# Delta-rule stage of a two-block transformer kernel: blockwise inverse by substitution, folded q norm, an explicit order of steps

## The reference, cut to what matters

```python
proj = h @ w_in                                   # q, k, v, z and the two gates of a head
qkv = silu(causal_depthwise_conv(qkv, conv_w))
q = l2_norm(q) * 128 ** -0.5
k = l2_norm(k)
lower = where(strict, beta * (k @ k.T) * decay, 0)
u, w = triangular_solve(I + lower, [v * beta, k * beta * exp(g)])
v_new = u - w @ S                                 # chunk by chunk, S is carried on
o = q_dec @ S + (q @ k.T * decay) @ v_new
S = S * g_last + k_dec.T @ v_new
out = (rms_norm(o, o_gain) * silu(z)) @ w_out
```

## Time and profile before

| | us |
|---|---|
| median of 3 runs | 1770.11 (1769.47 to 1771.78) |
| the profiled execution's own time | 1770.35 |
| its span, first to last instruction | 1768.1 |

### The profile page before, as it was taken

How to read it: one execution, slowest core, us unless ns; L and a number is a source line. 1 busy time by engine, 2 the same in 40 slices (tenths; PEclk the granted TensorE clock), 3 DMA queues, 4 the chain that set the end, 5 groups by cost and what they waited for, 6 DMA issues and landing times.

```text
span 1768.1 us, 21827 instructions
## 1 busy us (share of the span) xinstructions
PE 1674.7 (95%) x8436; PEld 1319.8 (75%) x8436; DVE 875.8 (50%) x1388; ACT 784.2 (44%) x1345; POOL 202.1 (11%) x233
## 2 busy tenths in 40 slices
PE   6799999999988899999999799999997999999998
PEld 4578888888877687677777588766675888888867
DVE  4745555555554535455555543544337532344346
ACT  3543543543543424565565632555544432243243
POOL 0111112102102200023232300000002000000011
PEclk9999999999999999999999999999998999999999
DMA  4111111111110232421222123211121333223321
GB/s 167 60 36 37 60 48 37 60 49 37 60 37 23 104 105 73 125 78 65 70 76 72 42 86 98 75 48 60 48 72 48 108 106 99 92 98 104 98 72 48
DMA packets 40165, 127.29 MB, mean 72 GB/s; under 512 B 4576, under 2 KB 9104, under 8 KB 40064
## 3 DMA queue, kind: packets, MB, share of 16 engines
q1 hardware_dynamic: 38112, 121.65, 20.3%
q0 software_dynamic: 1040, 3.27, 0.5%
q10 hardware_dynamic: 912, 0.99, 0.2%
HBM read 122.69 MB, written 2.15 MB: 71 GB/s over the span
## 4 chain that ended last, share of the span: by engine, by line
PE 82%; DVE 7%; ACT 7%; issue 3%; POOL 1%; DMA 0%; SPq 0%; ACTq 0%; DVEq 0%
PE ps L637 80%; ACT L L1528 3%; DVE wl L1720 2%; DVE L L2169 1%; PE ps L975 1%; PE ps L783 1%; DVE qkv L1756 1%; POOL h L2416 1%; ACT wh L1133 1%; DVE qb L1807 0%; ACT L L1480 0%; DMA wraw<-in_wa 0%; DVE mo L2292 0%; ACT xr L1397 0%; DVE U L2033 0%
## 5 line engine op out<-in xcount | busy, mean ns | idle before, releaser
L637 PE MATMUL ps<-xr,wh 128*128 128x512 f32 x2752 | 904.8, 410 | 15.4 <-DVE wl L1720 14.1
L637 PEld LDWEIGHTS ps<-xr,wh 128*128 128x128 f32 x2752 | 501.3, 190 | 143.7 <-issue 41.7
L637 PE MATMUL ps<-xr,wl 128*128 128x512 f32 x1376 | 542.3, 394 | 0.0
L1720 DVE TENSOR_TENSOR wl<-wraw,wh 128x1024 fp32r<-128x1024 f32 x214 | 261.4, 1236 | 152.7 <-ACT wh L1133 150.8
L637 PEld LDWEIGHTS ps<-xr,wl 128*128 128x128 f32 x1376 | 260.5, 189 | 57.3
L1133 ACT ACTIVATE wh<-wraw 128x1024 fp32r<-128x1024 f32 x214 | 220.4, 1048 | 20.1 <-PE ps L637 17.7
L637 PE MATMUL ps<-xm,wh 128*128 128x512 f32 x640 | 202.6, 398 | 11.3 <-DVE xm L2285 7.1
L637 PEld LDWEIGHTS ps<-xm,wh 128*128 128x128 f32 x640 | 121.8, 192 | 42.5 <-issue 9.2
L637 PE MATMUL ps<-xm,wl 128*128 128x512 f32 x320 | 126.3, 395 | 0.0
L2401 POOL TENSOR_SCALAR L<-L,m 128x256 f32<-128x256 f32 (+1 forms) x128 | 75.9, 614 | 325.3 <-DVE m L2184 325.3
L2345 POOL TENSOR_TENSOR Mm<-AT,masks 128x512 f32<-128x512 f32 x56 | 83.0, 1489 | 239.1 <-PE ps L637 122.6
(11 more groups left out here) (240 smaller groups left out, 1908.8 us busy)
## 6 DMA issues: line engine op xcount, KB each, us to landing
wraw<-in_wa SPq DMA_DIRECT2D x48, 512.0 KB, 3.2
wraw<-in_wb SPq DMA_DIRECT2D x32, 512.0 KB, 3.3
wraw<-in_wu SPq DMA_DIRECT2D x32, 512.0 KB, 3.2
wraw<-in_wd SPq DMA_DIRECT2D x32, 512.0 KB, 3.3
wraw<-in_wao SPq DMA_DIRECT2D x16, 512.0 KB, 3.3
wraw<-in_wbo SPq DMA_DIRECT2D x16, 512.0 KB, 3.3
wraw<-in_wc SPq DMA_DIRECT2D x16, 512.0 KB, 3.3
bias<-rel_rows SPq DMA_DIRECT2D x16, 256.0 KB, 3.7
```

Of the source, the lines that this page charges most:

```text
L637: return e.matmul(out, w, x, start=start, stop=stop, skip_group_check=True)
L1720: e.tensor_tensor(m.wl[:, i % N_SPLIT, :], m.raw[:, i % N_RAW, :], m.wh[:, i % N_SPLIT, :].bitcast(F), ALU.subtract).then_inc(s.wlo, 1)
```

## The change

1. The inverse. The diagonal 16x16 blocks are inverted by forward substitution, all 32 of them (8 a chunk, four chunks) at once and packed as [128, 4, 16]: DVE reduces the masked matrix to its diagonal blocks, 15 `stream_shuffle` instructions spread one row each over the partitions of its block, and POOL runs one copy and 15 times a product and a sum on a shrinking width 15 to 1, each waiting for the one before (`invert`, 31 instructions a head). DVE spreads the result out to U, and transposes it within blocks of 32 for T. Only the levels 16, 32 and 64 are left to PE; T behind the 32-level is made by PE's transposes and an ACT copy, and T behind the 16-level by DVE.
2. q is not normed. Its squared norm, scaled by `Q_SHARE`, is added to the output's sum of squares, which gives the same quotient; the two squares of the output are added on DVE, so one product with ones is left.
3. z is drained into the output's own place and run through Silu together with q, k and v of the next head; in the last head at the start of its recurrence.
4. The order. `weave` with written plans (`PLAN`, `STEADY`) takes the place of `merge` in the delta-rule stage: each entry is a step of prep (p), of recur (r) or of gates (g) and the gemm steps behind it. `PRODUCTS` moves the z products: z of heads 0 and 1 into round 1, then z of head i-1 behind head i's products.
5. The output products `ao` and `bo` begin inside the last two heads (pairs): the first two groups run side by side, slice by slice as the pieces are split (14 of their 16 slices each), the rest follows.
6. The start: ACT scales all of x before it squares it, DVE splits before it sums, the gates' weights are loaded and split early, the two chains of the gates alternate. SP looks one block less ahead, and its extra look-ahead at two stage borders is gone. `Ring.use` no longer begins with the bank that was used last.

The diff, cut to its core:

```diff
+PRODUCTS = {
+    1: (("head", 0), ("head", 1), ("z", 0), ("z", 1)),
+    2: (("head", 2),),
+    3: (("head", 3), ("z", 2)),
...
+    7: (("head", 7), ("z", 6)),
+    8: (("z", 7),),
+}
+PAIRED = (0, 2, 1, 3) + tuple(range(4, 16))
...
+def weave(g, order, parts, beside):
+    for name, n in order:
+        if name in parts:
+            next(parts[name], None)
+            if beside:
+                beside()
+        for _ in range(n):
+            next(g, None)
...
+    0: plan("g8 g2 g5"),
+    1: plan("p3 p2 p5 p0 p0 p1 p1 p0 p4 p3 p0 p3 p0 p6 p1 p4 p0 p2 p3 p3 p2 p4"),
+    HEADS: plan("r0 p0 r1 r2 p2 p1 p2 r2 r2 p0 p0 p0 r1 p1 p0 r2 p1 r2 r2 p2 p0 r2 p7 r0 p1 p4 p3 p2 p3 p2 p2 p1 p0"),
+    HEADS + 1: plan("r0 r0 r0 r4 r0 r0 r0 r0 r0 r3 r3"),
+}
+STEADY = plan("r0 p0 r2 p2 r2 p1 r2 p2 r0 p1 p1 p1 r0 p1 p1 r1 p4 r1 r2 p0 r2 p1 r7 p1 p0 p5 p2 p2 p3 p2 p2 p1 p4")
...
+    def pieces_out(name, out, lo, hi):
+        yield from split_pieces(name, lo, min(lo + 4, hi))
+        for i in range(lo, hi):
+            if i + 4 < hi:
+                yield from part(name, i + 4)
+            yield from take(out, 2)
...
+    out = gemm("ao", pair_groups("wao", 8), 2)
+    for i in range(1, HEADS + 2):
...
+        elif i == HEADS:
+            g = chain(products(i), pieces_out("split_o", out, 0, 12))
+        elif i == HEADS + 1:
+            g = pieces_out("split_o", out, 12, 14)
+        weave(g, PLAN.get(i, STEADY), parts, p.get("tap"))
+        drain(g)
...
     do("residual")
+    banks((4, 5, 6, 7, 0, 1))
+    drain(out)
     banks(WIDE)
-    drain(gemm("ao", pair_groups("wao", 8), 0))
...
+    out = gemm("bo", pair_groups("wbo", 8), 2)
     for j in range(16):
-        side = tiles(j + 2) if j < 14 else (split_pieces("split_ob", 0, 14) if j == 15 else None)
-        merge(side, 0.85, part("attend2", j), part("attend", j + 1) if j < 15 else None, lead=4)
+        side = tiles(j + 2) if j < 14 else pieces_out("split_ob", out, *((0, 8) if j == 14 else (8, 14)))
+        merge(side, 0.85 if j < 14 else 1.4 if j == 14 else 2, part("attend2", j),
+              part("attend", j + 1) if j < 15 else None, lead=4)
...
+    ("G", "ks", "kk", "qk", "kT", "v0", "v1", "P4", "U4", "P5", "U5", "T5", "P6", "U6", "w"))}
...
-        e.wait_ge(s.rec_a, REC_A * h + 6)
-        for j in range(2):
-            ins = mm(m.banks[5][:], m.ones, m.sqh[:, j, :], j == 0, j == 1)
+        e.wait_ge(s.rec_v, REC_V * h + 5)
+        mm(m.banks[5][:], m.ones, m.sqh[:, 0, :]).then_inc(s.rec_p, 1)
...
+        did(e.tensor_reduce(m.dc[:], m.Mm[:, 1].rearrange("p n (b c) -> p n c b", b=8), AX.X, ALU.add, negate=True))
+        yield
...
+        for r in range(15):
+            e.stream_shuffle(m.nb[:, r], m.dc[:].rearrange("p n c -> p (n c)"), [r] * 16 + [16 + r] * 16).then_inc(s.rows16, 1)
+            if r % 5 == 4:
+                yield
...
+        e.wait_ge(s.inv, N_INV * (h + 1))
...
+        did(e.tensor_tensor(U.rearrange("p n (b c) -> p n b c", b=8), m.uc[:].unsqueeze(2).to_broadcast([128, 4, 8, 16]),
+                            m.m16.rearrange("p (b c) -> p b c", b=8).unsqueeze(1).to_broadcast([128, 4, 8, 16]),
+                            ALU.mult))
...
+        did(e.transpose(m.Tm[:].rearrange("p n c -> p (n c)"), U.rearrange("p n c -> p (n c)")))
...
+    def invert(h):
...
+        did(e.tensor_copy(m.uc[:], m.unit.unsqueeze(1).to_broadcast([128, 4, 16])))
+        done += 1
+        for r in range(15):
+            w = 15 - r
...
+            e.wait_ge(s.rows16, 15 * h + r + 1)
+            e.wait_ge(s.inv, done)
+            did(e.tensor_tensor(part, nb[:, :, r + 1:], m.uc[:, :, r:r + 1].to_broadcast([128, 4, w]), ALU.mult))
+            e.wait_ge(s.inv, done + 1)
+            did(e.tensor_tensor(m.uc[:, :, r + 1:], m.uc[:, :, r + 1:], part, ALU.add))
+            done += 2
...
+    def gate_z(h):
+        for j in range(2):
+            z = m.XF[:, 16 + 2 * h + j, :]
+            e.wait_ge(s.adrain, z_drain(h, j))
+            e.activation(z, z, ACT.Silu).then_inc(s.za, 1)
...
-            load(i + N_RAW + 1)
+            load(i + N_RAW)
```

More of the change, by code:

```diff
@@ L41, in block_order @@
         out += [("wb", j), ("wb", 16 + j)]
-    out += [("wbo", b) for b in range(16)]
+    out += [("wbo", b) for b in PAIRED]
     for j in range(4):
@@ L90, in use @@
     def use(self, banks):
+        last = self.banks[(self.turn - 1) % len(self.banks)] if banks != WIDE else None
         self.banks, self.turn = banks, 0
+        if last == banks[0]:
+            self.turn = 1
     def next(self):
@@ L139, in chain @@
         yield from g
-def spread(g, every):
-    for _ in g:
-        for _ in range(every - 1):
-            yield "pass"
-        yield
 def take(g, n):
@@ L233, in flush, with products @@
                 pass
+    def products(i):
+        return chain(*(gemm(what, groups_of(what, h), 3 if (what, h) == ("head", 0) else 0, h) for what, h in PRODUCTS[i]))
     do("begin")
-    first = gemm("head", head_groups(0), 3, 0)
+    g = products(1)
     for _ in range(24):
-        next(first)
+        next(g)
     do("rms_x")
-    for i in range(HEADS + 2):
-        if i == 0:
-            second = gemm("head", head_groups(1), 0, 1)
-            merge(chain(first, take(second, 14)), 4, part("gates"), beside=p.get("tap"))
-            flush()
-            continue
-        banks(NARROW)
-        gen = [gemm("z", z_groups(i - 2), 0, i - 2)] if i >= 2 else []
-        gen += [gemm("head", head_groups(i), 0, i) if i > 1 else second] if i < HEADS else []
-        gen += [split_pieces("split_o", 0, 14)] if i == HEADS + 1 else []
-        merge(chain(*gen), FILL.get(i, 1.15), part("prep", i - 1) if i <= HEADS else None,
-              spread(part("recur", i - 2), 2) if i >= 2 else None, beside=p.get("tap"))
+    for _ in range(11):
+        next(g)
+    banks(EARLY)
+    weave(g, PLAN[0], {"g": part("gates")}, p.get("tap"))
+    out = gemm("ao", pair_groups("wao", 8), 2)
+    for i in range(1, HEADS + 2):
+        parts = {}
+        if i <= HEADS:
+            parts["p"] = part("prep", i - 1)
+        if i >= 2:
+            parts["r"] = part("recur", i - 2)
+            banks(NARROW)
+        if i in (2, 3, 4, 5, 6, 7):
+            g = products(i)
+        elif i == HEADS:
[4 more added lines that the diff above has]
+        drain(g)
         flush()
@@ L732, in rms_x @@
         clear[2] = [(s.nln, 1)]
-    @part
-    def gates():
         e.wait_ge(s.gate_v, 1)
@@ L797, in prep, with four_of @@
[L797 to L807 removed]
+        def four_of(name, w, x, *until):
+            end(name, four(begin(name), w, x), *until)
+            return idle(1)
@@ new lines, in turned_of @@
+        def turned_of(name, x, *until):
+            end(name, turn4(begin(name), x), *until)
+            return idle(1)
+        e.wait_ge(s.gate_v, 12)
+        yield from four_of("G", lambda n: m.gg[:, h, n:n + 1].to_broadcast([128, 128]), lambda n: m.triu,
+                           (s.prep_v, prep_v(h, "dv")), (s.prep_a, prep_a(h, "eb")))
+        begin("ks")
+        e.wait_ge(s.prep_a, prep_a(h, "sqk"))
+        end("ks", mm(m.banks[prep_bank(h, "ks")][:], m.ones, m.rq[:, 0, :]), (s.prep_a, prep_a(h, "lnk")))
@@ L811, in prep @@
             e.wait_ge(s.prep_a, prep_a(h, f"silu{2 + j}"))
[L812 to L822 removed]
+            yield from turned_of(f"v{j}", lambda n: v[:, ch[n]], (s.prep_a, prep_a(h, f"v{j}")))
@@ L823, in prep @@
+        yield from idle(5)
+        for i in range(4, 7):
+            if i == 6:
+                e.wait_ge(s.prep_a, prep_a(h, "T5"))
             else:
@@ L2472, in begin @@
             split(pace.upto(k // 2 + 1))
-    @part
-    def scale(to):
-        if to != "b":
-            split(pace.ahead(4))
     @part
```

500 lines of the change are left out of this document (253 added, 247 removed).

## The result

| | us |
|---|---|
| before, median (4 runs of this comparison) | 1770.82 (1769.47 to 1771.78) |
| after, median of 4 runs | 1714.24 (1713.80 to 1715.76) |
| ratio, 95% interval | 0.9683, 0.9666 to 0.9699 |
| the profiled execution's own time after, its span | 1715.76, 1714.0 |

The change makes the kernel 56.6 us faster. The forecast was 1664, a gain of 106, and its range ended at 1712, 2 us short.

What follows compares the result with a forecast made beforehand. PE, busy 95% of the span, bounds the kernel. Start and round 1 -0.6, round 2 -9.4, rounds 3 to 7 -50.4, rounds 8, 9 and `ao` -36, `bo` -10: -106.4 from 1770.35 gives 1664 us, range 1637 to 1712.

Steps and rivals of the forecast that it cites:

- a steady round above 60: Rounds 3 to 7: a round longer than 60 us would show the prediction wrong; 56.5 was forecast.
- kk waits: Prep, k's product with itself: PE waiting before it, ACT's chain to k's norm too late, would show the prediction wrong.
- PE waits 1 us: Steady rounds, before PE's level-16 inverse products: 13.2 us of cover left against a 14.2 us POOL chain, so 1 us wait.
- Levels 32 and 64 of the mask stand behind the 31 steps in POOL's queue, but P5 and P6 want them 6 us later: POOL's masks for the inverse's upper levels: queued behind the substitution, wanted 6 us later by PE's level-32 and level-64 products; no cost counted.
- DVE ... stays near 39 of 56.5: DVE in a steady round: ten operations of 0.69 a head go, about 7 us come; busy near 39 of 56.5, cost nothing.
- a bare link takes 1.86 ... 14.7: End of round 2, from the level-16 inverse to w, uncovered: links of 1.86 to 2.7 and others, together 14.7 us.
- G of head 0 at 57.7: Start: head 0's first prep product, for the decay matrix, begins at 57.7 us instead of 64.24, since the gate chains alternate.
- PE waits 6 us: Round 1, before the level-16 inverse: cover of only 6.6 us against a POOL chain of 12.6, so PE waits 6.
- theory 2: From the experiments, not the prediction: where PE waits, it is slowed as well, so a wait is paid twice.
- I take 10: Second output product: 28 of its 128 steps move into the last two attention pairs, where PE idles 11.2 us; gain 10.
- `ao` and rounds 8 and 9: Last two heads and first output product, begun early: together 144 us against 180.0 before.
- POOL's chain becomes the bound: Rival, chance 0.25: DVE's two-input operations lengthen the chain to 20 us, PE waits 7 in rounds 2 to 7; 1708.

Runs made afterwards that it cites:

- the late mask: Against the changed kernel, POOL cuts the 32-level's mask behind DVE's transposition, no longer beside DVE's U write: 1703.86 us, ratio 0.9618.
- z of head 1: Against the changed kernel, the 16 z gemm steps of head 1 move from round 1 to round 2: 1703.52 us, ratio 0.9616.
- the gates: Against the changed kernel, the gates begin 11 gemm steps earlier, ahead of head 0's evictions in DVE's queue: 1714.42 us, ratio 0.9682.
- the filled gaps: Useless PE products before the level-16 inverse in rounds 1 and 8 (22 and 20), run on the changed kernel only with the late mask, z of head 1, the gates: 1687.69 us.

## Why the prediction was wrong

The direction and the place were right: PE's work fell by near what was counted, and P4 waits for DVE's transposition. Of the signs that the prediction named as wrong, a steady round above 60 did not come (58.3), and kk waits in round 1 alone. What failed, by its steps:

- *Rounds 3 to 7, "PE waits 1 us".* The mechanism held, the size did not: 2.17 at P4 and 0.99 ahead of the sums' product in the head shown. Counted were 5.3 until the first shuffle is out, 14.2 for the chain and 1.8 behind it, 21.3 in all; measured 6.6 to POOL's first step, 16.1 and 2.6, 25.3 in all (263.96 to 270.58 to 286.68 to 289.25). The cover was longer too, 22.1 (25.3 less the two waits) instead of 20.3, so the wait grew by 2.1 and not by 4. A free step took some 0.37 from start to start (0.29 to 0.46) instead of 0.33, and the waiting beside DVE was about 5 instead of 4 (16.1 less 30 free steps at 0.37). Of the Trainium skill's figure, "GPSIMD Engine Reference", section 3.1, an estimate of 0.22 a step stood in the prediction; the trace has 0.21 at 128x4 and 0.29 at 128x60 for the operation itself. What the estimate lacked is the step's wait on its own predecessor.
- *"Levels 32 and 64 of the mask stand behind the 31 steps in POOL's queue, but P5 and P6 want them 6 us later"*, at nothing. The result is wanted late, but the operation runs at once, beside the U write, and cost 1.05 a head; the run that moved it gave 10.4 us. This is the dearest single line that was set to zero.
- *"DVE ... stays near 39 of 56.5"*, at nothing. The sum held (183.82 / 5 = 36.8 a round), but in the stretch ahead of the U write DVE's queue is as late as POOL's chain: without the chain the write began only 0.35 earlier. A queue that is idle for a third of a round can still be full where it matters.
- *Round 2, "a bare link takes 1.86 ... 14.7".* The links were priced from rows at the full clock. At the clock of 0.50 that followed PE's waits it was 21.3; with useless work in the gaps and the clock at 1.00 it was 15.4. The slow start of the next round (its w to w took 62.56 against 58.3) and part of the slow fours in rounds 1 and 8 are the same term. The run with the gaps filled gave 10.2 us.
- *Start, "G of head 0 at 57.7".* That the two chains alternate was taken as shorter; but the second gate step was put behind eight gemm steps' evictions, taps and low half on DVE. Mending it gave next to nothing by itself, so most of what is lost there is hidden by head 0's own convolution.
- *Round 1, "PE waits 6 us":* 7.66, and 1.64 and 1.27 ahead of kk and v, and a low clock behind P4 (0.63 from 100 to 105 us, a part of theory 2 that was not counted).
- *`bo`, "I take 10":* 3.6 by the run that undoes it. Idle PE time was counted as if anything could fill it; the work that could fill it had to be split by ACT and DVE, and the splits delayed what PE was waiting for.
- *`ao` and rounds 8 and 9* held better: 149.3 against 144, and 2.8 of the 5.3 are P4's wait (6.77 against the 4 counted); the early steps are worth 16.6.

Of the rivals, "POOL's chain becomes the bound" lay nearest in time (1708), but not by its price: its chain was to be 20 and the wait 7 a head. The time came from several smaller terms, the clock and DVE's queue among them, that no rival held; that it lies so near is luck.

Together the late mask, z of head 1, the gates and the filled gaps give back 26.5 of the 50.2 us by which the change missed the forecast. Of the 23.7 that are left, 6.4 are `bo`'s; no run takes the rest apart. Open are also what the two steps ahead of the sums' product cost by themselves, and how much of DVE's queue could be moved out of the stretch between kk and P5 without leaving work out.
